# Key norm and group norm of a recurrent mixer: eight-column sums and spreading products, or one product and wide reciprocals

## What is computed

```python
kk = _heads(k * k_k).astype(jnp.float32)
kk = kk / jnp.maximum(jnp.linalg.norm(kk, axis=-1, keepdims=True), 1e-12)
...
o = _wkv7_scan(rh, _heads(decay), kh, vh, kk, ah)
mu = jnp.mean(o, axis=-1, keepdims=True)
var = jnp.mean(jnp.square(o - mu), axis=-1, keepdims=True)
o = ((o - mu) * lax.rsqrt(var + GN_EPS)).reshape(h.shape[0], h.shape[1], D_RWKV)
o = (o * ln_g.astype(jnp.float32) + ln_b.astype(jnp.float32)).astype(h.dtype)
```

## Time and profile before

| | us |
|---|---|
| Median of 3 runs | 2043.44 (2042.44 to 2046.78) |
| Profiled execution | 2043.83 |
| its span | 2042.0 |
| TensorE busy | 1961.9 |
| VectorE busy | 974.6 |
| ScalarE busy | 779.6 |
| GpSimd busy | 918.8 |

### The profile page before, as it was taken

One profiled execution on the slowest core, in us unless ns is written; L12 is line 12 of the kernel. 1 busy time (PEld: TensorE's weight loads), 2 busy tenths in 40 slices (PEclk: granted clock), 3 DMA queues, 4 the chain that ended last, 5 costly groups with the idle time before them and its releaser, 6 DMA issues.

```text
span 2042.0 us, 44509 instructions
## 1 busy us (share of the span) xinstructions
PE 1961.9 (96%) x19112; PEld 1555.7 (76%) x19112; DVE 974.6 (48%) x1653; ACT 779.6 (38%) x1274; POOL 918.8 (45%) x750
## 2 busy tenths in 40 slices
PE   6989999999999999998999999999999999999997
PEld 5876667887788888886777677777787888888886
DVE  6333453232741322576677777777435266322312
ACT  4456664223432322443434334334245244322321
POOL 5333365444454545556443334333244445545542
PEclk9899999999899999998999999999999999999999
DMA  8420012533333333341111111111142332333331
GB/s 337 178 80 22 12 52 96 187 111 102 127 122 94 101 96 94 94 147 46 47 52 50 41 47 52 50 45 38 59 139 77 130 103 87 99 93 104 93 102 64
DMA packets 53075, 187.30 MB, mean 92 GB/s; under 512 B 6032, under 2 KB 7184, under 8 KB 52624
## 3 DMA queue, kind: packets, MB, share of 16 engines
q1 hardware_dynamic: 49104, 174.49, 26.9%
q10 hardware_dynamic: 3776, 9.96, 1.4%
HBM read 178.14 MB, written 6.29 MB: 90 GB/s over the span
## 4 chain that ended last, share of the span: by engine, by line
PE 88%; DVE 5%; issue 2%; ACT 2%; POOL 2%; DMA 0%; DVEq 0%; SPq 0%; ACTq 0%
PE psum L919 23%; PE psum L920 21%; PE psum L921 21%; PE psum L1072 2%; PE psum L1093 1%; PE psum L930 1%; PE psum L933 1%; PE psum L931 1%; POOL wlo L795 1%; PE psum L1078 1%; PE psum L1396 1%; PE psum L1393 1%; PE psum L1386 1%; DVE psum L2336 1%; PE psum L1332 1%
## 5 line engine op out<-in xcount | busy, mean ns | idle before, releaser
L795 POOL TENSOR_TENSOR wlo<-raw,whi 128x512 fp32r<-128x512 f32 x524 | 717.3, 1391 | 926.2 <-ACT whi L1562 926.2
L919 PE MATMUL psum<-ah,whi 128*128 128x512 f32 x1224 | 508.9, 416 | 1.8 <-POOL ah L805 1.2
L920 PE MATMUL psum<-ah,whi 128*128 128x512 f32 x1224 | 481.0, 393 | 0.0
L921 PE MATMUL psum<-ah,wlo 128*128 128x512 f32 x1224 | 480.7, 393 | 0.0
L1562 ACT ACTIVATE whi<-raw 128x1024 fp32r<-128x1024 f32 x262 | 275.8, 1053 | 321.6 <-PE psum L921 280.2
L919 PEld LDWEIGHTS psum<-ah,whi 128*128 128x128 f32 x1224 | 231.4, 189 | 61.3 <-issue 10.5
L921 PEld LDWEIGHTS psum<-ah,wlo 128*128 128x128 f32 x1224 | 231.5, 189 | 50.9
L920 PEld LDWEIGHTS psum<-ah,whi 128*128 128x128 f32 x1224 | 231.8, 189 | 44.3 <-issue 3.6
L919 PE MATMUL psum<-hidden,whi 128*128 128x512 f32 x472 | 183.8, 389 | 0.0
L921 PE MATMUL psum<-hidden,wlo 128*128 128x512 f32 x472 | 183.6, 389 | 0.0
L920 PE MATMUL psum<-hidden,whi 128*128 128x512 f32 x472 | 183.6, 389 | 0.0
(11 more groups left out here) (417 smaller groups left out, 2934.6 us busy)
## 6 DMA issues: line engine op xcount, KB each, us to landing
raw<-in_w SPq DMA_DIRECT2D x300, 512.0 KB, 3.6
raw_first<-in_w SPq DMA_DIRECT2D x14, 512.0 KB, 9.3
raw_ck<-in_w SPq DMA_DIRECT2D x8, 512.0 KB, 6.8
x<-in_x SPq DMA_DIRECT2D x4, 512.0 KB, 5.8
x_kept<-x ACTq DMA_DIRECT2D x1, 2048.0 KB, 10.1
ao_kept<-ao ACTq DMA_DIRECT2D x8, 256.0 KB, 2.0
aof<-ao_kept ACTq DMA_DIRECT2D x1, 2048.0 KB, 11.0
x<-x_kept ACTq DMA_DIRECT2D x1, 2048.0 KB, 8.1
```

The source lines that it names most:

```text
L795: pool.tensor_tensor(lo_weight(place(s))[:, c], raw_of(SPLITS[s])[:, c], hi_weight(place(s)).bitcast(F32)[:, c], ALU.subtract).then_inc(lo ...
L919: pe.matmul(dst, wh, h_, start=first, stop=False)
L920: pe.matmul(dst, wh, l_, start=False, stop=False)
L921: return pe.matmul(dst, wl, h_, start=False, stop=last)
```

## The change

The sum of squares becomes one product with all 128 columns of `heads` as the weights and `sq` as the moving operand: every channel gets the sum of its head at once, 128x512 in PSUM. The spreading products "kkb" and "gnb" are gone, and two of the waits with them. Clamp and root work on 512 columns (the group norm's clamp becomes the bias of the root), in `sq` itself. The reciprocal works on 512 columns too, in two halves of 256 with events of their own: "kkinv" 0 and 1, "gnr" 0 and 1. The multiplication reads the factor from `sq` in SBUF. Along with it, the list is changed: the halves lie in different slots, "gnend" moves from behind "ip" 2 to behind "iy" 3, the key's multiplication one slot later, and the taps of the convolution are dealt out in another way for the tiles from 1 on. The diff, cut to its core:

```diff
 def tile_ahead(j):
...
-            + v[2:3] + [("kk", j), ("lg2", j)] + v[3:] + [("kkss", j), ("kkinv", j)] + g[:1] + [("mix", j, 2)] + g[1:2] + [("kkb", j)] + g[2:3] + [("bonus", j)]
+            + v[2:3] + [("kk", j), ("lg2", j)] + v[3:] + [("kkss", j)] + g[:1] + [("mix", j, 2), ("kkinv", j, 0)] + g[1:2] + [("kkinv", j, 1)] + g[2:3] + [("kkb", j), ("bonus", j)]
 def first_tile():
...
-            + [("kk", 0), ("uput", 0), ("conv", 0, 2), ("lput", 1), ("kkss", 0)] + own1 + [("conv", 0, 2), ("kkinv", 0), ("conv", 0, 3), ("kkb", 0)]
-            + [("at", 0), ("re", 0)] + v + [("hidden", 1), ("conv", 0, 2), ("norm2", 0), ("norm2", 1), ("factor", 2), ("mix", 0, 2), ("lg2", 0)]
+            + [("kk", 0), ("uput", 0), ("conv", 0, 2), ("lput", 1), ("kkss", 0)] + own1 + [("kkinv", 0, 0), ("kkinv", 0, 1), ("conv", 0, 1), ("kkb", 0)]
+            + [("at", 0), ("conv", 0, 4), ("re", 0)] + v + [("hidden", 1), ("conv", 0, 2), ("norm2", 0), ("norm2", 1), ("factor", 2), ("mix", 0, 2), ("lg2", 0)]
-TAPS = ((1, 0), (2, 0), (1, 0), (2, 0), (0, 0), (0, 0), (2, 0), (1, 0), (2, 0), (0, 1), (0, 0), (1, 0), (0, 2), (4, 0), (2, 0))
+TAPS = ((2, 0), (2, 0), (2, 0), (0, 0), (0, 0), (0, 0), (2, 0), (2, 0), (0, 0), (0, 1), (0, 0), (1, 0), (0, 1), (2, 0), (2, 0))
 def rwkv_order():
...
-        out += [("akv", j, 0), ("akv", j, 1), ("opv", j, 0)] + ([("gnv", j - 1)] + held[1:] if j else []) + slot() + [("conv", j, 1 if j else 0), ("opv", j, 1)]
+        out += [("akv", j, 0), ("akv", j, 1), ("opv", j, 0)] + ([("gnv", j - 1)] + held[1:] if j else []) + slot() + [("conv", j, 4 if j else 0), ("opv", j, 1)]
         for lv in range(1, LEVELS):
             out.append(("ip", j, lv))
             if lv == 2 and j:
-                out += [("gnb", j - 1), ("gnend", j - 1)]
-            out += slot() + [("ix", j, lv)] + slot() + [("iy", j, lv)] + (slot() if lv in (1, 3) else [])
-            if lv == 3 and j:
+                out.append(("gnr", j - 1, 1))
+            out += slot() + [("ix", j, lv)] + slot() + [("iy", j, lv)]
+            if lv in (1, 3) and j:
+                out.append(("gnr", j - 1, 0) if lv == 1 else ("gnend", j - 1))
+            out += slot() if lv in (1, 3) else []
+            if lv == 4 and j:
                 out.append(("aoput", j - 1))
...
-    behind = [[("gnm", KT - 1)], [("gnv", KT - 1)], [("gnb", KT - 1), ("gnend", KT - 1)], [("aoput", KT - 1)], [("aoload", KT - 1)], []]
+    behind = [[("gnm", KT - 1)], [("gnv", KT - 1)], [("gnr", KT - 1, 0), ("gnr", KT - 1, 1)], [("gnend", KT - 1)], [("aoput", KT - 1)], [("aoload", KT - 1)], []]
 TensorE
                 elif kind == "kkss":
                     pe.wait_ge(kksq_ready, j + 1)
-                    for t in range(TT):
-                        mm = pe.matmul(b[:, 2 * t:2 * t + 2], sq[:, 0, t * P:t * P + P], heads[:, ::RN], start=True, stop=True)
-                elif kind in ("kkb", "gnb"):
-                    src = nrt if kind == "kkb" else gnt
-                    pe.wait_ge(nrm_ready if kind == "kkb" else gnr_ready, j + 1)
-                    for t in range(TT):
-                        for hh in range(2):
-                            mm = pe.matmul(b[RN * hh:RN * hh + RN, t * P:t * P + P],
-                                           src[:, 2 * t + hh:2 * t + hh + 1].to_broadcast([P, RN]), eye, start=True, stop=True)
+                    mm = pe.matmul(b, heads, sq[:, 0, :], start=True, stop=True)
 ...
                 elif kind == "gnv":
                     pe.wait_ge(gnsq_ready, j + 1)
-                    for t in range(TT):
-                        mm = pe.matmul(b[:, 2 * t:2 * t + 2], sq[:, 1, t * P:t * P + P], heads[:, ::RN], start=True, stop=True)
+                    mm = pe.matmul(b, heads, sq[:, 1, :], start=True, stop=True)
 ScalarE
                 elif kind == "kkss":
                     wait_emptied(act, f)
-                    act.activation(nrt[:, :], nrt[:, :], ACT.Sqrt).then_inc(kkroot_done, 1)
+                    act.activation(sq[:, 0, :], sq[:, 0, :], ACT.Sqrt).then_inc(kkroot_done, 1)
                 elif kind == "gnv":
-                    wait_emptied(act, f)
-                    act.activation(gnt[:, :], gnt[:, :], ACT.Sqrt).then_inc(gnroot_done, 1)
+                    wait_filled(act, f)
+                    emptied_by(act.activation(sq[:, 1, :], bank(f), ACT.Sqrt, bias=eps[:, 2:3], scale=1.0 / RN), f)
 VectorE
                 elif kind == "kkss":
                     wait_filled(dve, f)
-                    if j:
-                        wait_filled(dve, ("kkb", j - 1))
-                    emptied_by(dve.tensor_scalar(nrt[:, :], bank(f)[:, 0:2 * TT], KK_EPS * KK_EPS, None, ALU.max), f)
+                    emptied_by(dve.tensor_scalar(sq[:, 0, :], bank(f), KK_EPS * KK_EPS, None, ALU.max), f)
                 elif kind == "kkinv":
+                    half = slice(S // 2 * f[2], S // 2 * f[2] + S // 2)
                     dve.wait_ge(kkroot_done, j + 1)
-                    dve.reciprocal(nrt[:, :], nrt[:, :]).then_inc(nrm_ready, 1)
+                    dve.reciprocal(sq[:, 0, half], sq[:, 0, half]).then_inc(nrm_ready, 1)
                 elif kind == "kkb":
-                    wait_filled(dve, f)
-                    dve.wait_ge(kksq_ready, j + 1)
-                    emptied_by(dve.tensor_tensor(kk[:, :], kk[:, :], bank(f), ALU.mult), f)
+                    dve.wait_ge(nrm_ready, 2 * j + 2)
+                    dve.tensor_tensor(kk[:, :], kk[:, :], sq[:, 0, :], ALU.mult).then_inc(kkn_ready, 1)
                 elif kind == "gnv":
-                    wait_filled(dve, f)
-                    if j:
-                        wait_filled(dve, ("gnb", j - 1))
-                    emptied_by(dve.tensor_scalar(gnt[:, :], bank(f)[:, 0:2 * TT], 1.0 / RN, GN_EPS, ALU.mult, ALU.add), f)
-                    dve.wait_ge(gnroot_done, j + 1)
-                    dve.reciprocal(gnt[:, :], gnt[:, :]).then_inc(gnr_ready, 1)
+                    pass
+                elif kind == "gnr":
+                    half = slice(S // 2 * f[2], S // 2 * f[2] + S // 2)
+                    wait_emptied(dve, ("gnv", j))
+                    dve.reciprocal(sq[:, 1, half], sq[:, 1, half]).then_inc(gnr_ready, 1)
                 elif kind == "gnend":
-                    wait_filled(dve, ("gnb", j))
-                    emptied_by(dve.scalar_tensor_tensor(og, og, vcol("ln_x_g_2", j), bank(("gnb", j)), ALU.mult, ALU.mult), ("gnb", j))
+                    dve.wait_ge(gnr_ready, 2 * j + 2)
+                    dve.scalar_tensor_tensor(og, og, vcol("ln_x_g_2", j), sq[:, 1, :], ALU.mult, ALU.mult).then_inc(gn_done, 1)
```

More of the change, by code:

```diff
@@ L231 @@
 RKV_SLOT = {1: 0, 0: 1, 2: 0}
-IN_BANKS = ("lw2", "la2", "lg2", "kkss", "bonus", "tok", "inv", "akv", "ip", "ix", "iy", "jt", "jy", "tav", "st", "gnm", "gnv", "kkb", "gnb")
+IN_BANKS = ("lw2", "la2", "lg2", "kkss", "bonus", "tok", "inv", "akv", "ip", "ix", "iy", "jt", "jy", "tav", "st", "gnm", "gnv")
 BLOCKS = weight_blocks()
@@ L602, in build_program @@
             sw, cw, rate, kk = (work(n, S) for n in ("sw", "cw", "rate", "kk"))
-            nrt, gnt = work("nrt", 2 * TT), work("gnt", 2 * TT)
             bv = work("bv", 2 * S)[:, :].rearrange("p (i s) -> p i s", i=2)
@@ L797, in weights_ahead @@
                     low[0] += 1
-            for i, value in enumerate((EPS, LN_EPS)):
+            for i, value in enumerate((EPS, LN_EPS, GN_EPS)):
                 pool.memset(eps[:, i:i + 1], value).then_inc(eps_ready, 1)
@@ L870, in _ @@
                 elif kind == "at":
-                    wait_emptied(pool, ("kkb", j))
+                    pool.wait_ge(kkn_ready, j + 1)
                     pool.tensor_tensor(rate[:, :], kk[:, :], rate[:, :], ALU.mult).then_inc(pool_f, 1)
@@ L1595, in root @@
                 i = 1 if name == "conv" else 0
[L1596 removed]
+                act.wait_ge(eps_ready, 3)
                 wait_filled(act, ("ss", name))
@@ L2462, in _ @@
                 elif kind == "at":
-                    wait_emptied(dve, ("kkb", j))
+                    dve.wait_ge(kkn_ready, j + 1)
                     if j:
```

10 lines of the change are left out of this document (6 added, 4 removed).

## The result

The changed kernel takes 2056.99 us (median of 6 runs, 2052.85 to 2062.72), the kernel before 2046.26 beside it (6 runs, 2042.44 to 2047.81): ratio 1.0057, 95% interval 1.0041 to 1.0073, so it is slower. The profiled execution took 2056.64 us, its span is 2054.8: 12.8 more than that of before.

A forecast was written before the change was run, and what follows sets the result against it. TensorE was taken to bound the kernel. First tile +2.7, tile 0 +2.1, tiles 1 to 6 +9.8, tile 7 +1.9, last "gnb" -1.0: together +15.5, median 2058.5, likeliest 2058, range 2042 to 2065.

The forecast's parts named there:

- TensorE's own work: Spreading products "kkb" and "gnb" go: 1.03 us a group, 16 groups, at most 16.5 us saved.
- Place 1: Drain of "ip" 1, behind four more taps: TensorE's ix 1 waits 1.84 us in tiles 1 to 7.
- Place 2: "gnend" behind "iy" 3 meets GpSimd's `wlo`: "ip" 4 drained late, ix 4 waits 1.1 us in seven tiles.
- Place 3: Key's norm until chunk states: first state product waits for `pts`, 0.75 us in tiles 1 to 6, 3.1 in tile 0.
- the first rival: No collision with `wlo` at "gnend", VectorE gets in first: 7 x 1.1 us less, 2051; chance 0.17.
- First tile and tile 0: First tile: four taps ahead of the lora's second half, +2.7 us; tile 0: late `pts` less "kkb", +2.1.
- the rival of a cheap reciprocal: A reciprocal half takes near 0.42 us, so Place 3 goes and Place 1 stays: 2045; chance 0.13.
- the worse one with 2.4 us: Reciprocals of 2.4 us, and the scan meeting `wlo` delays the "iy" 2 drain: 2067; chance 0.10.
- that of lateness given back: All stalls end in slack where VectorE sets the pace, so the 16.5 us are gained: 2027; chance 0.10.

The follow-up runs named there:

- e9: e4 with the recurrent stage's weight loads (tiles from 1 on, and second gates) cut to 64 of 1024 columns: 2028.95 us, ratio 0.9914 to the kernel before.
- e10: The kernel before with the recurrent stage's weight loads (tiles from 1 on, and second gates) cut to 64 of 1024 columns: 2041.26 us, ratio 0.9974.
- e4: The changed kernel with three taps moved from ahead of the "ip" 1 drain to later slots, and "gnend" moved behind "ip" 3: 2038.27 us, ratio 0.9976.
- e1: The kernel before with four taps instead of one behind the slot ahead of "ip" 1: 2049.05 us, ratio 1.0026.
- e2: The changed kernel with one tap instead of four behind the slot ahead of "ip" 1, the others later: 2041.45 us, ratio 0.999 to the kernel before.
- e12: The changed kernel with GpSimd's two `wlo` instructions, for tiles from 1 on and second gates, on 32 columns instead of 512: 2053.03 us, ratio 1.0031.
- e8: e4 with the first tile's four taps moved behind the lora's second half: 2039.8 us, ratio 0.9968 to the kernel before.
- e5: The changed kernel with the second half of the group norm's reciprocal on 1 column, 255 left uninverted: 2055.83 us, ratio 1.0058 to the kernel before.
- e7: e4 with the last tile's "gnend" put back behind "iy" 3: 2040.81 us, ratio 0.9976 to the kernel before.

## Why the prediction was right

It had 2058, and the run gave 2057. The direction and the two waits that carry it were right, but that the sum comes out so close is luck: terms that were too large by 9 us stand against a clock that it didn't have, worth 6.7.

- **TensorE's own work:** the 1.03 us a group were right; 13 groups are gone in seven tiles. TensorE's busy time fell by 9.7 and not 16.5, since four stretches at half clock lengthen it by some 6.8. How much of it reaches the time is less sure: with the places' waits out of the way and the loads cut, e9 stands 12.3 us below e10 in the medians and 7.8 in the seven profiled tiles, where 13.4 are gone. With everything else in place e4 showed 5 of it.
- **Place 1:** 1.84 predicted, 1.93 measured, in all seven tiles. e1 makes such a wait alone, e2 takes it away. The reasoning from the timeline held, and so did its claim that the cost of a reciprocal doesn't enter.
- **Place 2:** 1.1 predicted, 1.04 to 1.22 measured, in six tiles of seven; e12 shows that GpSimd's `wlo` is the reason. Its bounds ran from 0 to 1.1, and the choice by the nearest row (the scan's) was good. In the seventh tile `wlo` came too late for it: the condition of the first rival, met once. An exclusive lock of the port pair held for a whole instruction is what the Trainium skill (SBUF — State Buffer, two separate sides) states; both engines' lengthened rows and e12 agree with it.
- **Place 3:** the mis-sized term. 0.75 was predicted in tiles 1 to 6, 0.08 came: 4 us too much. A half takes 1.75 us, below even the bound of 1.8, and the next instruction starts 1.67 behind its start, where the sum had 1.92; that is 0.5 for the two. `arow` behind them takes 1.19 us for 1.46, which the prediction didn't expect and no run explains. The copies `pts` end 0.49 us later in the tile than before, not 1.5. TensorE wants the product as early as predicted (0.2 us earlier in the tile than before), but that is luck: the sum left out place 2's 1.1 us there, and in tile 3 TensorE had made up 1.4 us on the way, in part in gaps that were longer before.
- **First tile and tile 0:** +4.8 predicted together, +1.7 measured, and 1.6 of that is the clock at 881.7, ahead of both. So the first tile gave -0.9 in place of +2.7: the 3.1 us of TensorE's wait for `lh` are there, as worked out, but they take the place of the wait for the bank that stands behind them (e8 removes them, and that wait grows by 3.0), and the missing "kkb" does give some 1.1 us (between 921 and 925 us). Tile 0 gave +1.1 for +2.1: the lateness costs 2.1 us and not 3.1.
- **What was missing:** the granted clock, 5.1 us in the tiles and 1.6 ahead of them. No step of the prediction had it, and none of the rivals.
- **The rivals:** the rival of a cheap reciprocal (0.42 us) is out by the row, and so is the worse one with 2.4 us; that of lateness given back by e1, where 5 of 8.0 us of waits show in the time, and by the books, where the waits at places 1 and 2 come out again in full in the tiles' length.

## What to carry to other kernels

On an engine that another one waits for, the place of work counted here and not its sum: 12.8 us of VectorE's work could go for nothing (e5), and four more taps of 0.78 us ahead of a drain cost 1.93 us seven times. Where products are replaced by longer work on another engine, try the arithmetic and the order apart: here the new arithmetic in a better order gains some 5 us (e4), and in the order that came with it loses 11. Whoever moves an operation to another place on an engine should look at what its neighbour on the same memory does just then. And a gap that the profile puts down to "issue" is to be laid beside the end of the drain that the product needs: in place 2 and in e7 it was a wait for VectorE, and in e4 it was none.
